# One core, two encoder layers: pair preparation one pair ahead with early stores, the scan written out, a norm's squares taken inside the embedding gate

## What is computed

```python
gate = sigmoid(rms_norm(h, ple_norm) @ ple_gate)        # end of layer 0
h = h + gate * (p @ ple_proj)
hn = rms_norm(h, mix_norm_pre[1])                        # start of layer 1
# RWKV-7, 16 heads of 64
r, k, v = xr @ w_r, xk @ w_k, xv @ w_v
decay = exp(-exp(-softplus(-(w0 + tanh(xw @ w1) @ w2)) - 0.5))
a = sigmoid(a0 + (xa @ a1) @ a2)
kk = k * k_k;  kk = kk / max(sqrt(sum(kk*kk per head)), 1e-12)
k_mod = k * (1 + (a - 1) * k_a)
S = S*decay_t + (S @ -kk_t) b_t^T + v_t k_t^T,  b = kk*a # per position
o_t = S r_t
o = groupnorm(o) + sum(r * k_mod * r_k) * v
```

## Time and profile before

| | us |
|---|---|
| median of 3 runs (lowest, highest) | 4018.39 (4010.32, 4018.71) |
| the profiled execution, its own time | 4018.97 |
| its span in the trace | 4017.2 |
| TensorE busy | 3646.6 (91%) |
| VectorE busy | 1540.8 (38%) |
| ScalarE busy | 856.4 (21%) |
| GpSimd busy | 207.1 (5%) |
| the embedding gate's last product ends, layer 1's norm begins its sums | 1769.7, 1773.7 |
| last unit of k ends; preparation's last wait ends | 2095.9, 2292.2 |
| the scan's first chunk of the loop to the last value | about 2340 to 2825 |

### The profile page before, as it was taken

The page is one execution under the profiler, slowest core; times in us unless marked ns, Lnnn a source line. Parts: engine busy times, 40 slices in busy tenths (PEclk is TensorE's granted clock), DMA queues, the critical chain, the costliest instruction groups (busy, mean ns, idle before and its releaser), DMA issues.

```text
span 4017.2 us, 66019 instructions
## 1 busy us (share of the span) xinstructions
PE 3646.6 (91%) x28466; PEld 3290.3 (82%) x28466; DVE 1540.8 (38%) x2029; ACT 856.4 (21%) x1134; POOL 207.1 (5%) x347
## 2 busy tenths in 40 slices
PE   6999999899999999889988688888698999999977
PEld 4997337799999999666987577787488999999967
DVE  3143554432212222536338644444734221222352
ACT  2000332210000010228225323233422000001020
POOL 0000000000000000001002211110100000000000
PEclk8999998899999999899998799889999999999989
DMA  2122002111121130124226621111411112113111
GB/s 89 60 77 80 22 22 82 71 43 47 42 82 53 42 129 29 49 75 171 87 104 254 237 86 52 46 42 34 147 60 54 42 39 80 60 44 120 42 39 69
DMA packets 79399, 301.59 MB, mean 75 GB/s; under 512 B 13560, under 2 KB 15880, under 8 KB 75192
## 3 DMA queue, kind: packets, MB, share of 16 engines
q0 software_dynamic: 36816, 174.51, 11.9%
q1 hardware_dynamic: 42368, 123.92, 9.9%
HBM read 217.29 MB, written 81.10 MB: 74 GB/s over the span
## 4 chain that ended last, share of the span: by engine, by line
PE 73%; DVE 7%; issue 2%; ACT 2%; DMA 1%; POOL 0%; DVEq 0%; ACTq 0%; POOLq 0%
PE ps L466 55%; DVE A L1537 2%; PE ps L912 2%; PE ps L903 2%; PE ps L480 2%; PE ps L440 1%; PE ps L773 1%; PE ps L863 1%; DVE H L1618 1%; DVE A_r L1594 1%; PE ps L498 1%; PE ps L926 1%; PE ps L929 1%; PE ps L878 1%; DVE B L1537 1%
## 5 line engine op out<-in xcount | busy, mean ns | idle before, releaser
L466 PE MATMUL ps<-H_r,W_r 128*128 128x364 f32 (+1 forms) x3192 | 705.8, 329 | 0.0
L466 PE MATMUL ps<-H_r,TM_r 128*128 128x364 f32 x2736 | 607.5, 330 | 21.6 <-DVE A_r L1594 18.0
L466 PE MATMUL ps<-A_r,TM_r 128*128 128x364 f32 x2736 | 606.2, 330 | 0.0
L466 PEld LDWEIGHTS ps<-H_r,W_r 128*128 128x128 f32 (+1 forms) x3192 | 556.3, 188 | 1.8
L466 PEld LDWEIGHTS ps<-H_r,TM_r 128*128 128x128 f32 x2736 | 475.9, 189 | 28.0 <-issue 19.8
L466 PEld LDWEIGHTS ps<-A_r,TM_r 128*128 128x128 f32 x2736 | 476.9, 189 | 0.0
L466 PE MATMUL ps<-B_r,DW_r 128*128 128x364 f32 x2112 | 408.8, 329 | 0.0
L466 PE MATMUL ps<-B_r,W_r 128*128 128x364 f32 x1824 | 404.8, 330 | 0.0
L466 PEld LDWEIGHTS ps<-B_r,DW_r 128*128 128x128 f32 x2112 | 358.8, 188 | 0.0
L466 PEld LDWEIGHTS ps<-B_r,W_r 128*128 128x128 f32 x1824 | 319.7, 190 | 0.0
L1800 DVE TENSOR_TENSOR TM<-ps,TM 128x1092 f32<-128x1092 f32 x44 | 57.0, 1296 | 444.1 <-PE ps L466 444.1
(11 more groups left out here) (303 smaller groups left out, 4444.5 us busy)
## 6 DMA issues: line engine op xcount, KB each, us to landing
W<-in_wgu SPq DMA_DIRECT2D x88, 512.0 KB, 3.6
H<-d_h POOLq DMA_DIRECT2D x3, 4368.0 KB, 23.1
W<-in_wdown SPq DMA_DIRECT2D x32, 384.0 KB, 3.1
W<-in_wrkv SPq DMA_DIRECT2D x24, 512.0 KB, 3.6
W<-in_wdown SPq DMA_DIRECT2D x32, 320.0 KB, 2.9
d_h<-H POOLq DMA_DIRECT2D x16, 546.0 KB, 3.0
d_y<-TM POOLq DMA_DIRECT2D x16, 546.0 KB, 3.4
A<-d_y POOLq DMA_DIRECT2D x16, 546.0 KB, 8.0
```

The source lines that it names most:

```text
L466: ins = nc.tensor.matmul(ps[0:cols, NCH * s + c, 0:CH], w[:, j * cols:(j + 1) * cols], x[k1][:, c * CH:(c + 1) * CH], start=(k1 == 0 and n ...
```

## The change

Three edits. The diff is cut to them; semaphore lists are left out.

1. **Norm.** In layer 0's gate VectorE squares each new tile of H into HSQ and adds it to HSUM, tiles 0 to 6; tile 7 is only squared. TensorE then needs two sums of three matmuls instead of eight. ScalarE's eight squares go.
2. **Preparation.** The loop is written out. The value product of pair i+1 is computed in pair i, the first before pair 0. ScalarE squares the key of pair i+1 in pair i, and takes two things from VectorE: the upper part of the weight, and the factor of k_mod. The maximum with the smallest norm becomes a bias of Ln and a minimum. GpSimd issues the stores of bk and ar as soon as the pair is done, ahead of the value tile and the sum, and waits for no landing; VectorE waits for the landing of the last pair's sum (`sum_out`) itself.
3. **Scan.** The loops of chunks 0 to 11 are written out on four engines.

```diff
@@ TensorE, start of layer 1 @@
-            norm_direct()
+            for n, x in enumerate((HSUM, HSQ)):
+                pe.wait_ge(S["h_sums"], n + 1)
+                for c in range(NCH):
+                    ins = nc.tensor.matmul(ps[:, NCH * s + c, 0:CH], k("ones"), x[:, c * CH:(c + 1) * CH],
+                                           start=(n == 0), stop=(n == 1))
@@ VectorE, ple_tiles @@
                         nc.vector.tensor_tensor(h, h, TM[:, j, :], ALU.add).then_inc(S["h_ready"], 1)
                         t.up("h_ready")
...
+                        dve.wait_ge(S["h_ready"], t.val("h_ready"))
+                        if last and j == 1:
+                            nc.vector.tensor_tensor(HSQ, h, h, ALU.mult).then_inc(S["h_sums"], 1)
+                        else:
+                            step(nc.vector.tensor_tensor(HSQ, h, h, ALU.mult))
+                            step(nc.vector.tensor_tensor(HSUM, HSUM, HSQ, ALU.add))
@@ TensorE, preparation @@
-                for u in range(4):
-                    pe.wait_ge(S["key_sq"], t.up("key_sq"))
-                    sums(k("pair"), TM[:, 1, :])
+            split_unit(xh, xlow[1], arriving=True)
+            for pair in range(NPAIR):
+                pe.wait_ge(S["key_sq"], pair + 1)
+                sums(k("pair"), TM[:, 1, :])
+                if pair + 1 < NPAIR:
                     split_unit(xh, xlow[1])
...
@@ ScalarE, preparation, per pair: Ln, Exp, expL, expnL, eLC, exp w, then @@
+                if pair + 2 < NPAIR:
+                    upper_value()
+                if pair + 1 < NPAIR:
+                    key_square(pair + 1)
+                    value_tile(pair + 1)
+                s, mm, rd = t.unit()
+                act.wait_ge(S["mm_done"], mm)
+                nc.scalar.activation(c3(TM[:, 2, :]), pset(s), ACT.Copy).then_inc(S[f"read{s}"], 1)
@@ VectorE, preparation, per pair @@
+                nc.vector.tensor_tensor_scan(cumL, reset, L["w"], 0.0, ALU.mult, ALU.add).then_inc(S["dve_p"], 1)
...
+                nc.vector.tensor_tensor(L["w"], cumL, L["w"], ALU.subtract).then_inc(S["dve_p"], 1)
...
+                nc.vector.tensor_tensor(L["k"], tmpK, L["k"], ALU.mult).then_inc(S["k_used"], 1)
+                dve.wait_ge(S["k_used"], pair + 1)
+                if pair:
+                    dve.wait_ge(S["sum_out"], 16 * pair)
+                stt(TM[:, 2, :], L["r"], v1("rk", pair), L["k"], ALU.mult, ALU.mult).then_inc(S["rk_ready"], 1)
...
+                stt(key, TM[:, 3, :], 1.0 / L2_EPS, key, ALU.min, ALU.mult).then_inc(S["rn_used"], 1)
...
+                step(nc.vector.tensor_tensor(tmpA, key, L["a"], ALU.mult))
+                if pair:
+                    dve.wait_ge(S["b_out"], 32 * pair)
@@ GpSimd, preparation @@
+            value_tile(0)
+            for i in range(NPAIR):
+                pool.wait_ge(S["pair_done"], i + 1)
+                pool.dma_start(d_bk[i], bk_out).then_inc(S["b_out"], 16)
+                pool.dma_start(d_ar[i], ar_out).then_inc(S["b_out"], 16)
+                t.skip(1)
+                if i + 1 < NPAIR:
+                    value_tile(i + 1)
                 s, mm, rd = t.unit()
                 pool.wait_ge(S[f"read{s}"], rd)
                 pool.dma_start(d_x["sum"][i], TM[:, 2, :]).then_inc(S["sum_out"], 16)
-                pool.wait_ge(S["sum_out"], 16 * i + 16)
-                pool.sem_inc(S["sum_stored"], 1)
-                pool.wait_ge(S["pair_done"], i + 1)
-                pool.dma_start(d_bk[i], bk_out).then_inc(S["b_out"], 16)
-                pool.dma_start(d_ar[i], ar_out).then_inc(S["b_out"], 16)
                 if i + 2 < NPAIR:
                     load_pair(i + 2)
-                pool.wait_ge(S["b_out"], 32 * i + 32)
-                pool.sem_inc(S["pair_stored"], 1)
@@ the scan, on each of four engines @@
-            with t.loop(3, ...):
-                for c in range(4):
-                    chunk(c)
-            for c in range(12, NCHUNK):
+            for c in range(NCHUNK):
                 chunk(c, prepare=c + 2 <= NCHUNK)
```

More of the change, by code:

```diff
@@ L55 @@
 DECAY = float(np.exp(-0.5))
+TINY = 1e-34
 SUMS = 8
@@ L830, in _ @@
             enter(t, "value")
[L831 to L836 removed]
+            split_unit(xh, xlow[1], arriving=True)
[3 more added lines that the diff above has]
+                if pair + 1 < NPAIR:
                     split_unit(xh, xlow[1])
[L838 to L839 removed]
+                pe.wait_ge(S["rk_ready"], pair + 1)
+                sums(k("pair"), TM[:, 2, :])
             for s in range(2):
@@ L1380, in _ @@
             act.wait_ge(S["xn_ready"], t.val("xn_tmp"))
[L1381 to L1416, removed]
@@ new lines, in upper_value, with value_tile @@
+            def upper_value():
+                slot, landed = t.chunk()
+                act.wait_ge(S[f"w{slot}"], landed)
+                nc.scalar.activation(wh_of(t), W[:, slot, 0:KT * P], ACT.Copy).then_inc(S["vh_ready"], 1)
+            act.wait_ge(S["xs2"], 96)
+            act.wait_ge(S["xs3"], 96)
+            def value_tile(i):
+                s, mm, rd = t.unit()
+                act.wait_ge(S["mm_done"], mm)
+                act.wait_ge(S[f"xs{i % 2}"], t.val(f"xs{i % 2}"))
+                t.up(f"xs{i % 2}", 32)
+                nc.scalar.activation(c3(B[:, 18 + i % 2, :]), pset(s), ACT.Copy).then_inc(S[f"read{s}"], 1)
@@ L2123, in _ @@
                 take_z(0, l, 1)
-            with t.loop(3, g_done=8, m_init=4, m_first=8, m_ready=8 * NL, z_done=8 * NL, st_done=8, st_read=8) as i:
-                for c in range(4):
-                    chunk(c, bass.ds(i * 4 + c, 1))
-            for c in range(12, NCHUNK):
+            for c in range(NCHUNK):
                 chunk(c, slice(c, c + 1), prepare=c + 2 <= NCHUNK)
@@ L2309, in _, with value_tile @@
             load_pair(1)
-            pool.sem_inc(S["sum_stored"], 1)
-            pool.sem_inc(S["pair_stored"], 1)
-            for i in range(NPAIR):
-                t.skip(1)
+            def value_tile(i):
                 s, mm, rd = t.unit()
@@ L2379, in _ @@
             pool.dma_start(H[:, :, :], d_h).then_inc(S["hs_in"], 16)
-            with t.loop(3, u_done=8, tok_done=8, zi0=96, zi1=96) as i:
-                for c in range(4):
-                    chunk(c, i * 4 + c)
-            for c in range(12, NCHUNK):
+            for c in range(NCHUNK):
                 chunk(c, c, prepare=c + 2 <= NCHUNK, load=c + 3 <= NCHUNK)
```

154 lines of the change are left out of this document (95 added, 59 removed).

## The result

The changed kernel takes 3997.3 us (median of 6, 3986.2 to 4002.6) where the kernel before takes 4016.5 beside it (6 runs, 4007.4 to 4021.6): a ratio of 0.995, 95% interval 0.9933 to 0.9968, so 19.2 us faster. The profiled execution took 3995.55 us with a span of 3993.9, 23.3 less than before.

A forecast was written before the change was run, and what follows sets the result against it. TensorE was taken to bound the kernel, leaving its chain at the norm's seam, the preparation (VectorE second) and the scan. The sum was 4018.97 - 14.6 + 5.9 - 6 = 4004.3 us, range 3988 to 4017.

The forecast's parts named there:

- Norm: -14.6: Seam after layer 0's gate: squares done early on VectorE let the sums end at 1775.7 instead of 1790.3, -14.6 us.
- The cover: Norm: 2.7 us extra VectorE work per tile delays a weight split wanted only one gate product (12.07 us) later.
- Preparation: +5.9: Preparation: pair period 21.9 us (20.5 to 23.3) against 21.1, so the end comes at 2298.1 instead of 2292.2, +5.9 us.
- The ring: Preparation: product into TM[2], pair done, bk, ar, value, sum landed, next product into TM[2]; period 21.9 us.
- VectorE's half: Preparation: VectorE's work from the product into TM[2] to the pair's last product takes 10.5 us.
- the half in the queue: Preparation: GpSimd's queue is served in order, so the sum lands 11.0 us after bk's issue, between 9.6 and 12.4.
- Scan: -6: Scan: writing out the loop removes two jumps and some half clock, 0.47 us for each of 12 chunks, -6 us.
- Rival (b): Scan: stays at full clock throughout, -19 us instead of -6, giving 3991 us; chance 0.07.
- Rival (c): Scan: straight code starves the instruction fetch, 31.3 us per chunk, +29 instead of -6, 4039 us; chance 0.06.
- The price of the jump: Scan: two loop jumps cost at least 2.5 us each, plus some half clock behind them.
- (a): Preparation: the queue isn't in order for stores, period 19.4 us, -10.6 us, giving 3987.8 us; chance 0.11.
- (d): Preparation: overlap works as meant, period about 17 us, -27 us, giving 3971 us; chance 0.03.

The follow-up runs named there:

- a queue of its own: Changed kernel with ScalarE issuing the store of the sum on its own queue, right behind the copy filling TM[2]: 3980.4 us, ratio 0.9908 to the kernel before.
- 128 increments: 128 idle semaphore increments on TensorE ahead of the scan: 3963.2 us on the kernel before, 3962.9 us on the changed kernel.
- VectorE's 32: Kernel before with 32 idle semaphore increments in VectorE's program ahead of the scan: 4016.1 us, ratio 0.9995.
- 32 increments: Kernel before with 32 idle semaphore increments in TensorE's program ahead of the scan: 4005.4 us against 4016.3, ratio 0.9971.
- the sum first: Changed kernel with GpSimd issuing the value tile and the sum ahead of bk and ar on the one queue: 4001.1 us, ratio 0.996 to the kernel before.
- the queue of its own with 128 increments: Changed kernel with the sum's store on ScalarE's queue and 128 idle semaphore increments on TensorE ahead of the scan: 3956.3 us, ratio 0.9862 to the kernel before.

## Why the prediction was right, and where it wasn't

**Norm: -14.6, measured -13.1.** The mechanism and the order are as forecast. The mis-sized term is the last sum: I took half of the 3.68 us for six matmuls, but six records are one sum (48 records for eight sums), and it starts on a TensorE at half its granted clock. 3.41 us instead of 1.9; the two handoffs were 0.06 and 0.04 us, 0.1 as assumed. The cover held: VectorE's extra squares delayed nothing that can be seen.

**Preparation: +5.9, measured +8.3 to +10.75.** The ring is there, and each of its marks: the first pair is done at 2120.3 (2138.0 less the 17.3 us by which the preparation starts earlier: 2120.7), the end behind the last pair takes 7.8 (7.75 forecast), VectorE's half 10.2 (10.5). The mis-sized term is the half in the queue: I took the middle, 11.0 us, of 9.6 to 12.4. The sum lands 12.3 us behind bk's issue in the median, at the upper bound, and in four of the eight pairs 12.5 to 13.4, beyond it. The row nearest to it was the landing of d_k with the weight's load beside it, and it should have been taken as it stood. From the first pair done to the last it is seven periods with a mean of 22.5, 157.6 us instead of 152.3: that is the 5 us. Of the Trainium skill's two rules ("DMA: Bandwidth & Descriptors") the one that descriptors of one queue start in order ("Two DMAs through the same engine are not ordered") agrees with the sum behind bk and ar, 10.1 us against 3.8 when first. The one that the DMA engines take turns between queues ("Queues, rings and completion order") these traces bear out only in part: a queue of its own brought the median to 5.6 us, but where the 2.2 MB were already in flight none of its packets moved for 4.5 us, and the store took 10.6.

**Scan: -6, measured -21.4, and for another reason.** The step that failed is "twelve chunks in the loop took 29.2 us each, the two straight ones 28.8": I read this as what chunks cost in the one form and the other, and priced only the jump. It is what they cost at this position of TensorE's code. With 128 increments a chunk of the same loop takes 24.7 us. Rival (b) had the size, and its reading of the granted clock was right, but writing out the code wasn't the cause: at 128 increments both forms are within 2.4 us. Rival (c), that straight code stalls in its fetch, is half true: at some positions there is a stall of up to 3.2 us per chunk, and it goes with a transfer of code, but that strikes the loop as well. The price of the jump, 2.5 us and some half clock, was too low: 6.6 us each at 128 increments, 13 for two; the straight code gives 11 of them back.

So the sign and the range came out by luck in good part. The norm gave 1.5 us less and the preparation cost 2.4 more than forecast, the unchanged stretches gave 1.8 and cost 2.2 and 2.4, and the scan gave 15.4 more, by a mechanism that the sum didn't have: 23.4 instead of 14.7. With 128 increments in both kernels the whole change moves the median by 0.3 us. Two sums of the prediction are off by a rounding, and nothing hangs on them: 8 x 5.3 is 42, not 43, and 0.53 with (a), (b) and (d) is 0.74, not 0.73.

## What to carry to other kernels

In a stretch of many short matmuls, read the idle time without a releaser first, and look whether its long pieces end some 2.7 us behind transfers on the instruction queue. If they sit at fixed places of the code and not only at jumps, the measured speed of the stretch belongs in part to the position of the code, and any edit ahead of it on that engine can move the time, here by 1%: compare versions by their stages, and put idle instructions ahead of the stretch in both before you believe a difference in it. Where somebody waits for a small store, neither issuing it first nor another queue is free: ask what the buffer behind the store that comes second is waiting for.

## What the runs showed of the hardware

- TensorE's program fixed the pace of the scan: 358.6 to 408.2 us for the same 14 chunks; in the kernel before, by idle instructions alone, 408.2, 397.5 and 361.0. VectorE's 32 changed nothing (406.6).
- TensorE's stalls of 1 us or more without a releaser, 108 in the 14 chunks of 14 traces, all end 2.2 to 3.7 us after the start of a 16 KB transfer on the instruction queue.
- A jump back on TensorE costs a stall of 3.1 to 4.3 us and, with half clock behind it, 6.6 us of a chunk at 128 increments; a stall inside straight code up to 3.2 us.
- More stall isn't always more time: with 32 increments the stalls sum to 44.7 us instead of 36.1, and the 14 chunks take 397.5 us instead of 408.2, with TensorE's waits for VectorE 11.9 us shorter and its busy time 5.7 us.
- The same 14 chunks with the same work have TensorE busy for 317.8 us at a granted clock of 1.00 and 349.1 at 0.90.
- The start of the program up to layer 0's last add, at 1761.1 to 1773.1 us, scatters by 12 us between two kernels whose code is the same there (the sum first, and the queue of its own with 128 increments): a difference of that size in one profiled execution, ahead of all edits, means nothing.
- A 546 KB store takes 3.2 us alone, 10.1 in the median behind 2.2 MB in its own queue, and up to 10.6 on another queue beside them.
